# One decoder trunk on one core: block 1's attention sums and gated output put ahead of the second head's queries, and its output product spread over steps 3 to 26 of the first gathers

## The reference

```python
def stick_breaking(q, k, v):          # per block of 128 queries
    z = jnp.einsum('bhqd,bhkd->bhqk', qi, kf) * scale
    log_stay = jnp.where(mask, jax.nn.log_sigmoid(-z), 0.0)
    suffix = lax.cumsum(log_stay, axis=3, reverse=True) - log_stay
    a = jnp.where(mask, jnp.exp(jax.nn.log_sigmoid(z) + suffix), 0.0)
    return jnp.einsum('bhqk,bhkd->bhqd', a, vf)

def layer_ab(h, ...):                 # stick-breaking and GLA side by side
    o_g = gla(...); o_g = o_g * lax.rsqrt(mean(o_g * o_g) + EPS) * gla_norm * silu(g_g)
    return jnp.concatenate([o_sb, o_g], axis=-1) @ w_out

def peer(h, w_q, subkeys, u_tab, v_tab):   # 8 heads, 16 experts per head and token
    q = (hf @ w_q).reshape(t_, PEER_HEADS, 2, PEER_QHALF)
    scores = jnp.einsum('thpd,hpnd->thpn', q, subkeys)
    top_s, top_i = lax.top_k(scores, 16)   # then the best 16 of the 16 x 16 pair sums
    gate = jax.nn.softmax(best_s, axis=-1)
    act = gelu(jnp.einsum('td,tkd->tk', xi, u_tab[idx]))
    return jnp.einsum('tk,tkd->td', gate * act, v_tab[idx])
```

## Time and profile before

| | us |
|---|---|
| median of three runs | 1610.74 |
| lowest and highest | 1608.64, 1611.03 |
| profiled execution, its own time | 1610.44 |
| its span, first to last instruction | 1608.7 |

### The profile page before, as it was taken

One profiled execution on the slowest core, in us unless ns is written; L12 is line 12 of the kernel. 1 busy time (PEld: TensorE's weight loads), 2 busy tenths in 40 slices (PEclk: granted clock), 3 DMA queues, 4 the chain that ended last, 5 costly groups with the idle time before them and its releaser, 6 DMA issues.

```text
span 1608.7 us, 14848 instructions
## 1 busy us (share of the span) xinstructions
PE 1435.1 (89%) x4450; PEld 706.9 (44%) x4450; DVE 980.8 (61%) x2487; ACT 668.4 (42%) x1841; POOL 656.8 (41%) x535
## 2 busy tenths in 40 slices
PE   7999999999957998998988999999889889797786
PEld 6656455565413333443343545445335345342222
DVE  1215578758748756753347756666456778777744
ACT  1524444534525334442244534343334454444433
POOL 1002344545424333353345333333334544556673
PEclk9999999999989999999999999999999999999999
DMA  7324999999999999999999999999999999999996
GB/s 289 131 106 177 400 412 393 422 420 421 420 422 421 413 422 421 421 422 421 421 420 413 421 421 421 421 421 379 422 421 408 423 420 411 421 421 421 421 422 274
DMA packets 86657, 626.57 MB, mean 389 GB/s; under 512 B 9761, under 2 KB 9905, under 8 KB 10673
## 3 DMA queue, kind: packets, MB, share of 16 engines
q0 software_dynamic: 73728, 536.90, 80.9%
q1 hardware_dynamic: 12672, 88.45, 13.5%
q10 hardware_dynamic: 176, 0.28, 0.1%
HBM read 624.54 MB, written 1.05 MB: 389 GB/s over the span
## 4 chain that ended last, share of the span: by engine, by line
PE 44%; DMA 32%; DVE 10%; ACT 6%; issue 4%; POOL 4%; SPq 0%; POOLq 0%; DVEq 0%; ACTq 0%
DMA ring<-in_peer_uv,experts 32%; PE acc L1597 23%; DVE ring L1238 6%; PE work L1376 5%; PE work L1359 4%; POOL ring L696 4%; PE work L1348 3%; PE acc L1560 1%; PE work L1391 1%; ACT diag L887 1%; ACT gelus L885 1%; PE work L1453 1%; PE work L1404 1%; ACT L884 1%; ACT gelus L884 1%
## 5 line engine op out<-in xcount | busy, mean ns | idle before, releaser
L1597 PE MATMUL acc<-ring,diag 128*128 128x512 f32 x2048 | 980.9, 613 | 154.7 <-ACT diag L887 153.0
L696 POOL DMA_INDIRECT ring<-in_peer_uv,experts x512 | 647.3, 1264 | 846.4 <-PE acc L1597 695.4
L1238 DVE CUSTOM_DVE_ANT_0 ring<-ring,h 128x1024 f32<-128x1024 f32 x512 | 624.4, 1226 | 428.2 <-DMA ring<-in_peer_uv,experts 414.7
L1597 PEld LDWEIGHTS acc<-ring,diag 128*128 128x128 f32 x2048 | 368.8, 192 | 684.3 <-ACT diag L887 343.1
L884 ACT ACTIVATE gelus<-dots 128x1 f32<-128x1 f32 x512 | 103.2, 202 | 690.2 <-DVE dots L1238 689.5
L887 ACT ACTIVATE diag<-ident,gelus 128x128 f32<-128x128 f32 x512 | 205.5, 401 | 16.7
L885 ACT ACTIVATE gelus<-gelus,gates 128x1 f32<-128x1 f32 x512 | 150.8, 295 | 16.6
L1376 PEld LDWEIGHTS work<-hT,weights 128*128 128x128 f32 x576 | 69.8, 192 | 16.3 <-issue 16.3
L1359 PE MATMUL work<-weights,hT 128*128 128x512 f32 x160 | 74.2, 592 | 0.0
L1376 PE MATMUL work<-hT,weights 128*128 128x128 f32 x576 | 70.1, 275 | 0.0
L884 ACT ACT_TABLE_LOAD x41 | 52.6, 1283 | 0.7
(11 more groups left out here) (234 smaller groups left out, 918.6 us busy)
## 6 DMA issues: line engine op xcount, KB each, us to landing
weights<-in_c_w_in SPq DMA_DIRECT2D x14, 1024.0 KB, 9.6
more<-in_c_w_in SPq DMA_DIRECT2D x11, 1024.0 KB
weights<-in_peer_w_q SPq DMA_DIRECT2D x10, 1024.0 KB, 9.8
weights<-in_ab_w_in SPq DMA_DIRECT2D x8, 1024.0 KB, 8.8
ring<-in_peer_uv,experts POOLq DMA_INDIRECT x512
weights<-in_ab_w_out SPq DMA_DIRECT2D x4, 1024.0 KB, 6.8
weights<-in_c_w_out SPq DMA_DIRECT2D x4, 1024.0 KB, 10.6
scores<-in_c_w_out SPq DMA_DIRECT2D x4, 1024.0 KB
```

Of the source, the lines that this page charges most:

```text
L696: pool.indirect_dma_start(ring[:, t % SLOTS, :], None, uv_rows, bass.IndirectOffsetOnAxis(ap=experts[:, b, step:step + 1], axis=0))\
L1238: nc.vector.tensor_tensor_reduce(out=ring[:, k, 0:D], in0=ring[:, k, 0:D], in1=h[:, b, :], scale=1.0, scalar=0.0, op0=ALU.mult, op1=ALU.ad ...
L1597: last = nc.tensor.matmul(acc[2 * b + n][:, :], diag[:, k, :], ring[:, k, D + n * CH:D + (n + 1) * CH], start=False, stop=True, skip_group ...
```

## The change

It changes PLAN and one index.

- Ahead of the gathers, the second head of block 0 (`scored(0, 0, 0, (1,))` and its DTAKE) comes behind the sums of batches 2 to 5, KV 1 and GLAREAD 1, not among them.
- The eight quarters of block 1's output product stand behind steps 3, 6, 9, 18, 20, 22, 24 and 26, not 2 to 9. OADD goes from step 10 to 27, the norm from 11 to 28, the transpose from 15 to 36.
- The queries of m = 1 start at step 10 with a gap of 1.75 (steps 10, 11, 13 and 15), not at 12 to 15; those of m = 2 at step 28 with a gap of 1.9 (28, 29, 31 and 33), not at 27, 29, 31 and 33.
- OUT takes the number of its weight chunk from a name, since chunk numbers between WOUT and the last OUT may now change.

```diff
--- before.py
+++ after.py
@@ -209,11 +209,11 @@
 
     out = [(0, ("SOUT", 1)), (1, ("STAKE", 1)), (1, ("GLASTAT", 1)), (2, ("GLAMEAN", 1)), (3, ("GLAOUT", 1)),
            (4, ("GLAT", 1)), (5, ("GLATAKE", 1)), (6, ("SPATIAL",)), (20, ("CAUSAL",))]
-    out += [(step, ("OUT", 1, n, q)) for n, steps in enumerate(((2, 3, 6, 7), (4, 5, 8, 9))) for q, step in enumerate(steps)]
-    out += ranked(0, 0, 0, 1) + [(10, ("OADD", 1))] + normed(11, "ffn0", 1)
-    out += [(15, ("TRANSPOSE", (1,), "ffn0")), (16, ("HTAKE", (1,), "ffn0"))]
-    return (out + projected(12, 0, 0, 1, 1) + ranked(20, 0, 0, 2) + ranked(26, 0, 0, 3)
-            + projected(27, 0, 0, 2) + ranked(38, 0, 0, 4, 2) + projected(38, 0, 1, 1, 5) + ranked(50, 0, 0, 5, 2)
+    out += [(step, ("OUT", 1, n, q)) for n, steps in enumerate(((3, 6, 9, 18), (20, 22, 24, 26))) for q, step in enumerate(steps)]
+    out += ranked(0, 0, 0, 1) + [(27, ("OADD", 1))] + normed(28, "ffn0", 1)
+    out += [(36, ("TRANSPOSE", (1,), "ffn0")), (37, ("HTAKE", (1,), "ffn0"))]
+    return (out + projected(10, 0, 0, 1, 1.75) + ranked(20, 0, 0, 2) + ranked(26, 0, 0, 3)
+            + projected(28, 0, 0, 2, 1.9) + ranked(38, 0, 0, 4, 2) + projected(38, 0, 1, 1, 5) + ranked(50, 0, 0, 5, 2)
             + projected(56, 0, 1, 2, 3) + projected(68, 0, 0, 3, 1.5) + ranked(77, 0, 0, 6) + projected(76, 0, 1, 0, 4)
             + ranked(85, 0, 0, 7, 2) + projected(91, 0, 1, 3, 4) + ranked(97, 0, 1, 0, 2) + ranked(108, 0, 1, 1, 2)
             + ranked(120, 0, 1, 2))
@@ -235,9 +235,9 @@
            ("TRANSPOSE", (0,), "ffn0"), ("HTAKE", (0,), "ffn0")]
         + scored(0, 0, 0, (0,)) + [("DTAKE", 0, 0, 0, (0,)), ("STICKZ", 4), ("STICKZ", 5), ("SOFT", 2, 3, 4, 5)]
         + ranked_now(0, 0, 0)
-        + [("SOFTLN", 2, 3, 4, 5), ("GV", 1), ("PROJV", 1), ("LOG", 2, 3, 4, 5)] + scored(0, 0, 0, (1,))[:-1]
-        + [("STICKE", 2), ("STICKE", 3), ("KV", 1), ("QDOT", 0, 0, 0, (1,)), ("DTAKE", 0, 0, 0, (1,)),
+        + [("SOFTLN", 2, 3, 4, 5), ("GV", 1), ("PROJV", 1), ("LOG", 2, 3, 4, 5), ("STICKE", 2), ("KV", 1), ("STICKE", 3),
            ("STICKE", 4), ("STICKE", 5), ("GLAREAD", 1)]
+        + scored(0, 0, 0, (1,)) + [("DTAKE", 0, 0, 0, (1,))]
         + gather_with(0, 0, parts_of_layer0())
         + gather_with(0, 1, trunk_for(0, 1.9, Z_ORDER[0]), rest_of_layer0())
         + gather_with(1, 0, ranks_for(0), trunk_for(1, 1.6, Z_ORDER[1], {4: (0, 2), 0: (0, 3)}))
@@ -353,6 +353,8 @@
 QUERIES = {}
 for _kind, _args, _at in walk():
     BANKS[_kind, *_args] = _at.bank
+    if _kind == "WOUT":
+        OUT_CHUNK = _at.chunk
     if _kind == "QPROD":
         QUERIES[*_args,] = len(QUERIES) % 3
 
@@ -1555,7 +1557,7 @@
 
                     b, n, q = args
                     own_copies(BANKS["GLAT" if q >= 2 else "SOUT", b], 1)
-                    wt = await_chunk(pe, at.chunk - 2 + n, (q // 2,))
+                    wt = await_chunk(pe, OUT_CHUNK + n, (q // 2,))
                     for k in range(q * KT // 4, (q + 1) * KT // 4):
                         last = nc.tensor.matmul(acc[2 * b + n][:, :], mixT[:, k, b * P:(b + 1) * P], wt[k],
                                                 start=(k == 0), stop=(k == KT - 1))
```

## The result

| | median us | ratio to before | 95% interval |
|---|---|---|---|
| before (12 runs) | 1610.26 | | |
| changed kernel (12 runs) | 1614.2 | 1.0029 | 1.0021 to 1.0036 |
| changed kernel, a second time (9 runs) | 1615.05, before there 1611.17 | 1.0024 | 1.0013 to 1.0034 |

The changed kernel is slower by 0.24 to 0.29%, 3.9 to 4.7 us, and both intervals lie above 1. I had forecast 1609.3 in a range of 1605.8 to 1612.5: no change, with a small gain. Its profiled execution took 1617.74 us (span 1616.0), at the slow end of its runs (1610.99 to 1617.74), so the excess of its span (7.3 us) is more than the typical one, and I read places from it and sizes from the ratios.

The account below looks back on a forecast made before the run. Moved bytes bound the kernel behind the first 160 us, leaving only DMA shortfall to win or add: +1.6 (start) - 1.3 (B) + 0.1 (C) - 1.7 (D) = -1.3 us, forecast 1609.3 us, range 1605.8 to 1612.5.

Parts of the forecast that it names:

- The start, 6 and 7 early: Ahead of step 0: transfers 6 and 7 go out near 151.9 and 154.8, 4 us earlier each; counted as nothing.
- The start, step 0 later: Step 0 starts at 161.45, not 159.87, behind the queries' wait, score copy and gelu table load: +1.6 us.
- Rival 1: Early transfers and the spread both pay, with step 0 not later: -5.0 us, 1605.7 us; chance 0.17.
- rival 4: ScalarE held behind its table load by about another load's length: +1.3 us, 1610.6 us; chance 0.04.
- Steps 1 to 19: From step 5 at 178.7, TensorE's own work sums to QDOT of step 17 at 211.6; terms -1.3 and +0.1 us.
- B: 182 to 190 us, TensorE full: the DMA's shortfall of 1.3 us was to go, -1.3 us.
- C: 220 to 236 us: shortfall of 1.0 us, replaced by 1.1 us from late transfers in steps 10 to 17, +0.1 us.
- Steps 20 to 38: Ranking with the add and norm in its middle; step 38's tile at 272.1, not 273.46; term -1.7 us.
- D: 256 to 280 us, after ranking: shortfall of 2.7 us, of which 1.0 was taken to stay, -1.7 us.
- my sign of being wrong: The forecast is wrong if, among other signs, step 38's tile comes before 270 or after 274.5 us.
- rival 2: Add in the middle of ranking stalls VectorE, 256 to 280 shortfall kept: +4.7 us, 1615.4 us; chance 0.11.
- rival 3: Weights of queries m = 2 come too late, waiting for step 18: about +2.5 us, 1613 us; chance 0.02.

Follow-up runs that it names:

- order_only: The kernel before with only the new order ahead of the gathers, output product still at steps 2 to 9; 1612.62 us, 1.0012 of before.
- spread_only: The changed kernel with before's order ahead of the gathers, so only the output product and what follows it move; 1611.62 us, 1.0007 of before.
- idle_filled: The changed kernel with output product pieces at steps 2, 3, 9, 18 and 4, 5, 22, 26; 1611.17 us, 1.0008 of before.
- gains_at_27: The changed kernel with the products for the norm's gain vectors behind step 27, not 29; 1614.87 us, 1.0031 of before.
- copy_behind_0: The changed kernel with ScalarE's copy of the second head's scores behind step 0's gelu and diagonal; 1613.24 us, 1.0017 of before.
- third_at_12: The changed kernel with the last piece of the output product's first half at step 12, not 18; 1614.87 us, 1.0031 of before.
- spare_work: The changed kernel with two unused TensorE products behind step 2 and two behind step 5; 1613.61 us, 1.0024 of before.

## Why the prediction was wrong

**The start, 6 and 7 early: right.** Transfers 6 and 7 went out at 151.78 and 154.74 (151.9 and 154.8), and nothing came of it.

**The start, step 0 later: right in cause, short in size.** Rival 1, which had step 0 in time, is ruled out. QDOT's wait is 0.52 us; the copy ends at 159.36, the load follows at 159.37, the diagonal ends at 161.63. Step 0 is 22.04 us behind the first transfer, and was 20.08: +2.0, and not +1.6. It works as a shift of 2.1 us at step 8 and 1.9 us in the time of order_only. The shortfall grew by 2.9 us in 156 to 168 (2.2 in the second profile), since I took the gap as moved and unchanged. Before, transfer 8 was issued while the DMA was still at work on 6 and 7, which had gone out 4 us later; now it is issued into a queue that is empty from about 162.3, and this window of the changed kernel shows how long that takes:

```profile
164.00:168.00 4.00, 3.53 (x34) 2.05 (x30) 1.75 (x6) 2.29 (x12) 1.46 (x1) 1.00 0.36 59
```

Transfer 8 is issued at 164.44, yet the DMA moves 59 GB/s until 168. I had counted 2 us from an issue to full rate; here it is some 3.5. The Trainium skill, page "ScalarE: Activation LUTs", section "What ACT_TABLE_LOAD costs", adds 1.4 us of drain to a load. None shows in this trace: the copy ends 0.01 us ahead of the load and the gelu begins 0.01 us behind its end, at 160.66. So rival 4 had nothing to stand on.

**Steps 1 to 19: this is the step that failed.** I wrote "from there I add TensorE's own work to QDOT at step 17", from step 5 at 178.7. Step 5 is at 178.90. But step 6 is at 183.03, where my sum has it at 180.4: it waits 2.14 us for a diagonal, as VectorE must first finish the GLA copy and the last ranking part. The dot product begins at 180.75, the diagonal at 182.57:

```profile
177.87 0.69 DVE L1192 TENSOR_TENSOR mixT<-work,consts 128x512 f32<-128x512 f32 x1 [1.30 <-PE work L1306]
...
180.75 1.23 DVE L1240 CUSTOM_DVE_ANT_0 ring<-ring,h 128x1024 f32<-128x1024 f32 x1
```

The same step stood at 181.27 in before and at 181.22 in spread_only, with and without a product of OUT ahead of it:

```profile
181.27 1.98 PE L1597 MATMUL acc<-ring,diag 128*128 128x512 f32 x4
```
```profile
181.22 1.98 PE L1599 MATMUL acc<-ring,diag 128*128 128x512 f32 x4 [2.14 <-ACT diag L889]
```

So the places of steps 2, 3, 5 and 6 are set by ScalarE and VectorE (the row of step 3 names no engine; the same row of spread_only, at 170.17, names ACT's diagonal). In before, three pieces of OUT at steps 2, 4 and 5 stood in those waits and cost nothing by step 6. Moved out, they bought no time there, and stand now at steps 18 to 26, where TensorE is busy for 16.00 of 16 us and each costs it 1.72 us. The lower clock at steps 6 and 7 added (3.17 - 1.88) + (2.43 - 1.88) = 1.8 us in this profile. QDOT came at 216.10 and not 211.6; the wait (2.6) and the clock (1.8) are the difference. That is still earlier than in before, where it is 80.7 us behind the first transfer (76.5 now). But before's queue had 4 MB of weights, 10 us, to move in that time, and the changed kernel's has none of them. So a shortage shows between 190 and 220 that before did not have, and it takes both to make it: the pieces out of the waits, and the loads put off.

I had -1.3 us for B and +0.1 for C, -1.2 together. In spread_only they are +0.4 (182 to 190), +3.3 (190 to 220) and -1.0 (220 to 236), so +2.7, and in the changed kernel's second profile +3.9. That is a miss of 3.9 to 5.1 us, most of what separates -1.3 from +3.9 to +4.7. idle_filled shows it from the other side: pieces put back in the waits bring 2.6 to 3.4 us.

**Steps 20 to 38: right in the cost, wrong in the times.** D is 0.1 us in spread_only, with 0.7 us in 280 to 300, and nothing in the changed kernel's second profile (422 GB/s); I had taken 1.0. In the first profile D is 2.6 us, behind long products at 245.74 and 249.32. The tile of step 38 is at 280.71, and 276.96 in the second profile, not at 272.1: my sign of being wrong, a tile after 274.5, came true. VectorE waited 2.62 us at the add (3.0) and 5.09 at the vectors (1.3; 2.07 in the second profile). Taking the second wait away brought nothing in the time (gains_at_27); the first was not taken away by itself.

**The rivals.** The time was nearest to rival 2, but not by its mechanism, which had D kept and two waits of VectorE on top: D went, and the waits did not decide. Of rival 3 nothing shows: the first tile that uses the late weights, at 249.32, has no wait in front of it. The loss had the sign of a case I did not have, work taken out of waits.

The sum by the terms of the two halves is +2.1 (start) + 2.7 (B and C) - 1.9 (D) = +2.9 us, and by the windows of the changed kernel's second profile +2.2 + 3.9 - 2.7 = +3.4 us. The ratios say 3.9 to 4.7, so about 1 us is not accounted for. The second profile has 1 us more in B and C than spread_only has. The lower clock near step 6 is the likely reason, since spread_only lacks it, but no run shows that by itself.

## What to carry to other kernels

Before work is spread from a dense stretch to a later one, look at what ends each wait in the dense stretch: an engine that is full there may be full because it fills time that other engines set. Look as well at which loads the moved work lets start, and whether the queue has enough else to move until then. Take the work out on paper and walk the chain of the other engines step by step; only what the chain then gets earlier is a gain, and each piece moved to where the engine is the limit costs that engine its full length. A head start for a transfer brings nothing if the next one in the queue waits for something that the same edit makes later.

## What the runs showed of the hardware that I had not expected

The granted clock of TensorE fell in stretches where the engine only had waits of 1 to 2.8 us between products. Two windows of the changed kernel's first profile:

```profile
184.00:188.00 4.00, 4.00 (x7) 1.68 (x6) 4.00 (x9) 3.05 (x12) 1.02 (x1) 0.61 1.00 416
...
244.00:248.00 4.00, 2.26 (x3) 1.18 (x4) 3.90 (x13) 2.62 (x8) 1.50 (x1) 0.64 1.02 426
```

The clock went to 1.2 GHz for a part of them (2.4 GHz is 1.00): it was 0.50 from 184 to 187, and from 246 to 251. TensorE had waited 1.81, 1.07 and 2.14 us before steps 3, 5 and 6, and 2.84 us before step 28. Near step 6 it fell in all five profiles with the changed order and these steps empty (both of the changed kernel, copy_behind_0, third_at_12, gains_at_27), not in that of spread_only with the same waits, and in none where work filled them. Near step 28 it came and went between two profiles of the same kernel, and it fell there in spread_only, copy_behind_0 and spare_work too (0.84, 0.63 and 0.57 in 244 to 248).

The indirect transfer takes long to start from an empty queue. Behind the issue at 164.44, which itself takes 1.46 us, nothing was moved until 166, then 131 and 106 GB/s in the next two microseconds, and 418 from 168 on. In before the first transfer, issued at 139.79, moved nothing until 141, then 98 and 246 GB/s, and 418 from 143 on.

The part ahead of the gathers, the same instructions in the same order, took 137.0 to 137.6 us in four profiles and 138.9 to 139.8 in the others. A comparison of two single spans of this kernel is worth no more than that.
